# Attention scores from hi and lo parts, wide projections, and a modulation vector's row sums begun two heads earlier

## The chip, the cores and the metric

The kernel runs on one core of a Trainium2 chip as one launch. The metric is the device time of that launch in microseconds (us). The engines are PE (TensorE: matmuls, with the weight loads in a row PEld of their own), DVE (VectorE), ACT (ScalarE), POOL (GpSimd) and SP (SyncE), which here only issues DMAs. Each engine runs its own instruction list in order; between engines the kernel sets and waits for semaphores.

## The reference

Two transformer blocks on `x` of 256 tokens x 1024 features, all in float32. What is computed, cut to what matters here:

```
# block 1
sh1, sc1, g1, sh2, sc2, g2 = split(silu(c) @ w_mod + b_mod, 6)      # c: 1024 values, w_mod: 1024 x 6144
hx = rms_norm(x, norm1_g) * (1 + sc1) + sh1 ; hc the same from ctx (256 tokens)
q, k, v, u, g = split(hx @ w_in) ; kc, vc from hc                   # 8 heads of 128, 2 key heads
q, k = rope(head_rms(q)), rope(head_rms(k))
attn = softmax(q @ [kc, k].T / sqrt(128)) @ [vc, v]                 # per head: 256 x 512 scores
y_a  = attn @ w_attn_out
h    = a * sigmoid(b), a, b = split(u)                              # 512 channels
y_b  = silu(layer_norm(depthwise_conv31(h))) @ w_conv_out
x    = x + g1 * ((sigmoid(g_a) * y_a + sigmoid(g_b) * y_b) @ w_out)
x    = x + g2 * conv_glu_ffn(rms_norm(x, norm2_g) * (1 + sc2) + sh2)
x    = rms_norm(x, final_g)
# block 2
h = h + 0.5 * rms_norm(swiglu(rms_norm(h)))
q_a, k_a, v_a, q_b, k_b, v_b = split(rms_norm(h) @ w_in_2)          # 8 heads of 64 each
h = h + rms_norm([norm(stick_breaking(a)), norm(chunk_band(b))] @ w_out_2)
h = h + 0.5 * rms_norm(swiglu(rms_norm(h)))
h = h + rms_norm((p @ w_ple_proj) * sigmoid(h @ w_ple_gate))
```

## The kernel before

**Products from parts.** A float32 matrix is split in a high part (a cast to the matmul type fp32r) and a low part (the float32 value minus the high part). A product is then three fast matmuls: hi x hi, hi x lo, lo x hi. For a weight chunk ACT makes the high part (`whi`, L1348) and DVE the low part (`wlo`, L1812, behind the cast); three buffers of each rotate. A few matmuls still run on plain float32 operands: the head scores (L957, `QT` x `KT`), the values (L978), transposes, and the modulation chunks (L765).

**The stream.** All large weights come in 164 chunks of 1 MB (128 x 2048 float32) through a ring of four slots, `raw0` to `raw3`. The list `STREAM` (L99 to L111) sets their order. SP issues the loads in that order (`ring`, L454): the load of chunk c waits until chunk c-4, its predecessor in the slot, is used up (`slot_free`, L447), and every later load stands behind it in SP's list. What frees a slot depends on the kind of chunk (L422 on): the DVE split (`lo_done`) for a weight chunk, the matmuls (`mod_used`, `acc_ready`) for a modulation chunk, and DVE's row sums (`mod_dot`) for a chunk of `scale2`.

**Stages.** q, u, kv and g0 (projections of block 1); eight heads; the rest of the merge (`attnout0` to `attnout3`, `g1b`, `wout`); up0, down0, up1, down1; qa, ka, va, vb, qb, kb0, kb1 with the two attentions of block 2; wout2, up2, proj, down2, gate. In PE's program a head is: scores, the values of the head before, a chunk of the modulation block `modB` (in heads 0 to 4 one, in head 7 three: `MOD_PER_HEAD`, L67), one feature tile of g (`tiles_stage`, L694), the transposes of the probabilities (`prob_transposes`, L960). The layer norm of the conformer branch is cut over heads 5 and 6: `ln_mean` on PE, then DVE's subtraction of the mean (L2113, `ln_c`), ACT's square, `ln_var` on PE in head 6 behind its scores and values (L998), rsqrt on POOL, a diagonal on DVE (L2118, `ln_diag`), its broadcast on PE (`ln_broadcast`, L1002), DVE's multiplication (L2123, `ln_n`), ACT's affine step and silu, and the cast `cvt_hi` and subtraction `cvt_lo` (L2094) in head 7, which `conv_products` (L1015) multiply.

**DVE in the heads** (L2087 on): two row maxima (L2090), taps of the depthwise convolution (`conv_taps`, 124 in all, in units of one instruction), two reciprocals of the row sums (L2099), more taps, the low part of the last head's values (`pv_lo`, L2074), the split of the next g chunk (`splits_to`). The taps stand wherever DVE would have had room: `conv_taps(2, 7, 8, 12)` between the units of kv, then up to 16 in each head until they are used up.

**The second scale.** `sc2` is not multiplied on PE. POOL loads `c` to all partitions (`c_row`, L592); ACT takes its sigmoid; DVE multiplies (L2139); then `mod_dots` (L1911) forms for each half of a `scale2` chunk a product and its row sum in one instruction (L1919), eight in all, four chunks in the stream just ahead of `attnout1`, `wout` 0, `wout` 3 and `up0` 0.

**Projections of block 2.** `project2` (L1130) uses `tiles_stage`: for each of two chunks eight k steps of two output tiles of three parts, 48 matmuls of 256 columns; the result stands in one PSUM bank and ACT copies it (`qk_out`, L1672).

## Time and profile before

| | us |
|---|---|
| time, median of 3 runs (lowest, highest) | 981.22 (981.05, 981.88) |
| the profiled execution: its own time | 981.24 |
| its span, first to last instruction in the trace | 979.3 |
| what lies around the span | 1.9 |
| PE busy | 959.9 (98%) |
| DVE, ACT, POOL busy | 690.7 (71%), 484.2 (49%), 56.7 (6%) |
| granted TensorE clock, mean (1 is full) | 0.999 |
| from HBM | 188.35 MB, 193 GB/s over the span |

PE is busy nearly throughout; the slices of the page show tenths, and PE stands at 9 in all but the first and the last. DVE's low slices lie in the later stages; in the first third, where the heads are, its slices read 8 and 9. The chain that ended last is made of matmuls. A busy share says nothing of what a stage waits for: an engine that is 71% busy over the span can be the last one in one stage.

### The profile page before, as it was taken

To read this page: it belongs to the slowest core of one execution; us is meant where nothing else is said; L and a number is where in the kernel's file an instruction comes from. 1 tells how busy PE (TensorE), PEld (TensorE's weight loads), DVE (VectorE), ACT (ScalarE), POOL (GpSimd) and SP (SyncE) were. 2 spreads that over 40 slices of the span, in tenths; PEclk is the share of its full clock that TensorE was granted. 3 is DMA by queue.
4 is the path that set the end of the run, shared out by engine and by line. 5 is a ranking of instruction groups with operands and counts; after the bars stand their busy time and mean duration, and the time that the engine had idled before them with its cause. 6 is when DMAs were issued, how large, how long until landed. Compare 5 with 4: busy or idle time off the path is not lost.

```text
span 979.3 us, 14504 instructions
## 1 busy us (share of the span) xinstructions
PE 959.9 (98%) x5720; PEld 824.2 (84%) x5720; DVE 690.7 (71%) x895; ACT 484.2 (49%) x644; POOL 56.7 (6%) x92
## 2 busy tenths in 40 slices
PE   7999999999999999999999999999999999999997
PEld 4697788788988888889888888898988988888885
DVE  3689998479879999757777764465555667776454
ACT  3565466664355555324545433258853454443343
POOL 0251000000000000010000000101001000000000
PEclk9999999999999999999999999999999999999999
DMA  9954254466475555943665555183421654555511
GB/s 379 394 212 169 103 218 154 167 248 231 154 298 195 212 193 208 326 174 119 247 245 205 184 207 210 44 306 137 171 87 44 237 215 172 213 212 182 207 44 43
DMA packets 27842, 190.12 MB, mean 194 GB/s; under 512 B 3120, under 2 KB 3376, under 8 KB 5776
## 3 DMA queue, kind: packets, MB, share of 16 engines
q1 hardware_dynamic: 26192, 184.23, 50.8%
q0 software_dynamic: 1456, 5.12, 1.7%
q8 instruction: 36, 0.59, 0.2%
q14 instruction: 14, 0.11, 0.0%
q10 hardware_dynamic: 144, 0.07, 0.0%
HBM read 188.35 MB, written 1.05 MB: 193 GB/s over the span
## 4 chain that ended last, share of the span: by engine, by line
PE 52%; DVE 1%; POOL 0%; ACT 0%; issue 0%; DVEq 0%; POOLq 0%; ACTq 0%
PE acc L1085 15%; PE acc L1088 8%; PE acc L672 6%; PE acc L674 6%; PE acc L673 6%; PE acc L814 3%; PE acc L675 1%; PE acc L677 1%; PE acc L676 1%; PE acc L797 1%; PE acc L1234 0%; DVE X L2326 0%; DVE XN L1838 0%; DVE XN L1843 0%; PE acc L1147 0%
## 5 line engine op out<-in xcount | busy, mean ns | idle before, releaser
L1812 DVE TENSOR_TENSOR wlo<-raw,whi 128x2048 fp32r<-128x2048 f32 x135 | 308.3, 2289 | 145.5 <-ACT whi L1348 145.4
L1348 ACT CAST whi<-raw 128x2048 fp32r<-128x2048 f32 x139 | 263.2, 1906 | 126.1 <-PE acc L674 84.0
L1085 PE MATMUL acc<-x_parts,whi 128*128 128x512 f32 x960 | 301.8, 396 | 0.0
L1088 PEld LDWEIGHTS acc<-x_parts,wlo 128*128 128x128 f32 x960 | 180.3, 188 | 42.6
L1088 PE MATMUL acc<-x_parts,wlo 128*128 128x256 f32 x960 | 188.7, 278 | 0.0
L1085 PEld LDWEIGHTS acc<-x_parts,whi 128*128 128x128 f32 x960 | 146.2, 189 | 0.0
L672 PE MATMUL acc<-whi,h_hi 128*128 128x512 f32 x264 | 103.0, 390 | 0.0
L674 PE MATMUL acc<-whi,h_lo 128*128 128x512 f32 x264 | 102.7, 389 | 0.0
L673 PE MATMUL acc<-wlo,h_hi 128*128 128x512 f32 x264 | 102.7, 389 | 0.0
L675 PE MATMUL acc<-x_parts,whi 128*128 128x256 f32 x288 | 83.2, 289 | 0.0
L677 PE MATMUL acc<-x_parts,wlo 128*128 128x256 f32 x288 | 81.5, 283 | 0.0
L676 PE MATMUL acc<-x_parts,whi 128*128 128x256 f32 x288 | 81.5, 283 | 0.0
L2240 DVE TENSOR_REDUCE FULL<-acc 128x512 f32<-128x1024 f32 x60 | 73.0, 1216 | 0.0
L672 PE MATMUL acc<-whi,x_parts 128*128 128x512 f32 x168 | 67.8, 403 | 2.5 <-issue 0.8
L674 PE MATMUL acc<-whi,x_parts 128*128 128x512 f32 x168 | 65.6, 390 | 0.0
L673 PE MATMUL acc<-wlo,x_parts 128*128 128x512 f32 x168 | 65.6, 390 | 0.0
L814 PE MATMUL acc<-FULL,raw 128*128 128x128 f32 x512 | 58.8, 275 | 0.0
L675 PEld LDWEIGHTS acc<-x_parts,whi 128*128 128x128 f32 x288 | 55.2, 192 | 4.1 <-issue 3.9
L814 PEld LDWEIGHTS acc<-FULL,raw 128*128 128x128 f32 x512 | 58.1, 192 | 0.5 <-DVE FULL L1882 0.2
L674 PEld LDWEIGHTS acc<-whi,h_lo 128*128 128x128 f32 x264 | 49.6, 188 | 10.3
L673 PEld LDWEIGHTS acc<-wlo,h_hi 128*128 128x128 f32 x264 | 49.6, 188 | 10.2
L672 PEld LDWEIGHTS acc<-whi,h_hi 128*128 128x128 f32 x264 | 49.6, 188 | 10.0
(297 smaller groups left out, 1220.4 us busy)
## 6 DMA issues: line engine op xcount, KB each, us to landing
raw<-in_stream SPq DMA_DIRECT2D x164, 1024.0 KB, 4.8
early<-in_early SPq DMA_DIRECT2D x8, 1024.0 KB, 13.4
X<-in_x SPq DMA_DIRECT2D x2, 512.0 KB, 4.5
G<-in_ctx SPq DMA_DIRECT2D x1, 1024.0 KB, 21.2
...
```

Source lines behind the costliest of these rows:

```text
L672: pe.matmul(out, xh, wh, start=start, stop=False)
L673: pe.matmul(out, xh, wl, start=False, stop=False)
L674: return pe.matmul(out, xl, wh, start=False, stop=stop)
L675: pe.matmul(out, wh, xh, start=start, stop=False)
L676: pe.matmul(out, wh, xl, start=False, stop=False)
L677: return pe.matmul(out, wl, xh, start=False, stop=stop)
L814: mm = pe.matmul(acc[:, BANK[i], o * T + t * P:o * T + (t + 1) * P], w[:, k, o * P:(o + 1) * P], FULL[:, k, t * P:(t + 1) * P], start=(k = ...
L1085: pe.matmul(acc[:, BANK[i + q] + o, :], w[0][:, k, o * P:(o + 1) * P], xs[:, k, :], start=(k == 0), stop=False)
L1088: mm = pe.matmul(acc[:, BANK[i + q] + o, T:2 * T], w[1][:, k, o * P:(o + 1) * P], xhi[:, k, :], start=False, stop=(k == KD - 1))
L1348: act.copy(whi[si_slot][:, :], raw[raw_slot][:, :]).then_inc(s["hi_done"], 1)
L1812: dve.tensor_tensor(wlo[slot][:, :], raw[raw_slot][:, :], whi[slot][:, :], ALU.subtract)\
L2240: dve.tensor_reduce(dst.rearrange("p (o n) -> p o n", o=2), parts, AX, ALU.add)\
```

## The change

1. **Scores from parts.** ACT casts `QT` to `side_hi` in two instructions and writes the keys straight to a high part (`KTh`, laid over `cvt_hi`); DVE makes the low parts in two (`q_lo`) and four (`k_lo`) instructions, between taps. `scores` calls `product`, three matmuls for each one before, and waits for `q_lo` and `k_lo`. Ten of the taps before head 0 move into the heads.
2. **Head 0.** ACT copies head 0's transposed probabilities before it casts the g3 chunk, not behind.
3. **silu(c).** In place of the sigmoid behind the heads, ACT takes exp(-c) in head 2 and DVE in head 5 adds 1, takes the reciprocal of 128 x 1024 values, and multiplies by c, ahead of the subtraction of the mean.
4. **Row sums of scale2.** The four chunks stand ahead of `convout1`, `modB.5`, `attnout1` and `wout` 0; the row sums are taken in head 6 (two, one on each side of the multiplication L2123), in head 7 (two), behind `branch_b` and behind `attnout1`.
5. **Merge.** The splits of `attnout0` and `attnout1` stand further ahead, and the diagonal of the gate moves from ahead of `attnout0`'s merge to behind it.
6. **Wide projections** for ka, qb and kb0 (five chunks): the high weight is multiplied with both parts of x at once (512 columns), the low weight with the high part (256 columns), in two banks; ACT copies one half and DVE adds the other (`qk_rest`).

```diff
-for _name, _chunks in (("scale2", (("attnout1", 0), ("wout", 0), ("wout", 3), ("up0", 0))),
+for _name, _chunks in (("scale2", (("convout1", 0), ("modB.5", 0), ("attnout1", 0), ("wout", 0))),
...
+            pool.wait_ge(s["q_lo"], 2)
+            pool.dma_start(bc[:, 1, :], bcast(a["c_row"], D)).then_inc(s["c_in"], 16)
             pool.wait_ge(s["ln_ve"], 1)
...
             def scores(h):
-                        pe.wait_ge(s["q_t"], 8)
+                        pe.wait_ge(s["k_lo"], 4)
...
-                    pe.matmul(tp[:, t, :], QT[:, h, t * P:(t + 1) * P], KT[:, h // 4, :], start=True, stop=True)\
-                        .then_inc(s["sc_ready"], 1)
+                    pe.wait_ge(s["q_lo"], h // 4 + 1)
+                    product(tp[:, t, :], side_hi[:, h, t * P:(t + 1) * P], side_lo[:, h, t * P:(t + 1) * P],
+                            KTh[:, h // 4, :], KTl[:, h // 4, :], True, True, True).then_inc(s["sc_ready"], 1)
...
+            def wide_stage(si, i, n=None):
...
+                    for o in range(2):
+                        pe.matmul(acc[:, BANK[i] + o, :], w[0][:, k, o * P:(o + 1) * P], xs[:, k, :], start=(k == 0),
+                                  stop=False)
+                    for o in range(2):
+                        mm = pe.matmul(acc[:, BANK[i] + o, T:2 * T], w[1][:, k, o * P:(o + 1) * P], xhi[:, k, :],
+                                       start=False, stop=(k == KD - 1))
...
+            for j in range(2):
+                act.copy(side_hi[:, 4 * j:4 * j + 4, :], QT[:, 4 * j:4 * j + 4, :]).then_inc(s["q_hi"], 1)
...
-                if h < 7:
+                if 0 < h < 7:
                     splits_to(SPLIT["g2"] + h + 2)
...
+                if h == 0:
+                    splits_to(SPLIT["g2"] + 2)
+                if h == 2:
+                    act.wait_ge(s["c_in"], 16)
+                    act.activation(XN[:, 0, :], bc[:, 1, :], ACT.Exp, scale=-1.0).then_inc(s["c_sig"], 1)
...
+                    act.wait_ge(s["sc_ready"], TT * NH)
                     act.copy(cvt_hi[:, :, :], QT[:, 0:4, :]).then_inc(s["ln_hi"], 1)
...
-                conv_taps((2, 7, 8, 12)[u - 4])
+                if u < 7:
+                    conv_taps((2, 7, 6)[u - 4])
+                if u == 5:
+                    k_lo(4)
+                    k_lo(5)
+            conv_taps(2)
+            q_lo(0)
+            conv_taps(2)
+            k_lo(6)
+            k_lo(7)
+            q_lo(1)
...
                 if h == 5:
+                    dve.wait_ge(s["c_sig"], 1)
+                    dve.tensor_scalar(XN[:, 0, :], XN[:, 0, :], 1.0, None, ALU.add).then_inc(s["c_sig"], 1)
+                    dve.wait_ge(s["c_sig"], 2)
+                    dve.reciprocal(XN[:, 0, :], XN[:, 0, :]).then_inc(s["c_sig"], 1)
+                    dve.wait_ge(s["c_sig"], 3)
+                    dve.tensor_tensor(bc[:, 1, :], bc[:, 1, :], XN[:, 0, :], ALU.mult).then_inc(s["c_row"], 1)
                     bank_ready(ACC["ln_mean"])
...
-            splits_to(SPLIT["g2"] + 9)
-            dve.wait_ge(s["c_sig"], 1)
-            dve.tensor_tensor(bc[:, 1, :], bc[:, 1, :], XN[:, 0, :], ALU.mult).then_inc(s["c_row"], 1)
+            splits_to(SPLIT["attnout0"] + 1)
             pv_lo(NH - 1)
             mod_out("modB")
-            splits_to(SPLIT["attnout0"] + 1)
-            dve.wait_ge(s["mod_out"], MOD_N["modB"])
-            diagonal(xn2[:, D:2 * D], 0)
+            splits_to(SPLIT["attnout0"] + 2)
             branch_b(2)
-            dve.wait_ge(s["c_row"], 1)
-            mod_dots("scale2", 0)
             branch_b(3)
+            mod_dots("scale2", 2)
...
+                if j == 0:
+                    dve.wait_ge(s["mod_out"], MOD_N["modB"])
+                    diagonal(xn2[:, D:2 * D], 0)
```

**Order, DVE before head 0.** Before, from the last rotation of a key unit to the reciprocals of head 0 (L2010 and L2017 belong to the unit, L2048 is a tap, L1812 the split of the g2 chunk, L2090 the row maxima):

```order
L2048 SCALAR_TENSOR_TENSOR XN<-conv_x,vt,XN 128x256 [waits conv_dve] x8
L2010 TENSOR_TENSOR FULL<-acc,small 128x256 [waits q_rot,q_ri]
L2017 TENSOR_TENSOR FULL<-FULL,G 128x256 [waits q_tps,q_norm]
L2048 SCALAR_TENSOR_TENSOR XN<-conv_x,vt,XN 128x256 [waits conv_dve] x12
L1812 TENSOR_TENSOR wlo3<-raw0,whi3 128x2048 [waits hi_done]
L2090 TENSOR_REDUCE small<-acc 128x1 [waits sc_ready] x2
L2048 SCALAR_TENSOR_TENSOR XN<-conv_x,vt,XN 128x256 [waits conv_dve] x4
L2099 RECIPROCAL small<-small 128x1 [waits p_exp] x2
```

After, the same stretch (L2101 is a tap, L2123 `q_lo`, L2129 `k_lo`, L1862 the split, L2166 the row maxima):

```order
L2063 TENSOR_TENSOR FULL<-acc,small 128x256 [waits q_rot,q_ri]
L2070 TENSOR_TENSOR FULL<-FULL,G 128x256 [waits q_tps,q_norm]
L2101 SCALAR_TENSOR_TENSOR XN<-conv_x,vt,XN 128x256 [waits conv_dve] x2
L2123 TENSOR_TENSOR side<-QT,side 128x4x256 [waits q_hi]
L2101 SCALAR_TENSOR_TENSOR XN<-conv_x,vt,XN 128x256 [waits conv_dve] x2
L2129 TENSOR_TENSOR cvt_lo<-acc,cvt_hi 128x2x128 [waits q_t] x2
L2123 TENSOR_TENSOR side<-QT,side 128x4x256 [waits q_hi]
L1862 TENSOR_TENSOR wlo3<-raw0,whi3 128x2048 [waits hi_done]
L2166 TENSOR_REDUCE small<-acc 128x1 [waits sc_ready] x2
L2101 SCALAR_TENSOR_TENSOR XN<-conv_x,vt,XN 128x256 [waits conv_dve] x4
L2176 RECIPROCAL small<-small 128x1 [waits p_exp] x2
```

Twelve taps in a row ahead of the split have become four, with two `q_lo` and two `k_lo` among them.

**Order, DVE in heads 5 and 6.** Before, from the split at the end of head 5 (L1812) over `ln_c` (L2113), head 6's maxima and reciprocals, the copy of the variance (L2106) and the split of the g7 chunk to the multiplication `ln_n` (L2123):

```order
L1812 TENSOR_TENSOR wlo1<-raw3,whi1 128x2048 [waits hi_done]
L2113 TENSOR_TENSOR XN<-XN,acc 128x1024 [waits acc_ready]
L2090 TENSOR_REDUCE small<-acc 128x1 [waits sc_ready] x2
L2099 RECIPROCAL small<-small 128x1 [waits p_exp] x2
L2074 TENSOR_TENSOR side<-acc,side 128x256 [waits a_hi]
L2106 COPY small<-acc 128x2 [waits acc_ready]
L1812 TENSOR_TENSOR wlo2<-raw0,whi2 128x2048 [waits hi_done]
L2118 TENSOR_SCALAR XN<-consts,small 128x128 [waits ln_r]
L2118 TENSOR_SCALAR XN<-consts,small 128x128
L2123 TENSOR_TENSOR XN<-XN,acc 128x1024 [waits ln_c,acc_ready]
```

After (L1862 is the split, L2190 to L2194 the three steps of silu(c), L2196 `ln_c`, L2201 the diagonal, L1968 a row sum):

```order
L1862 TENSOR_TENSOR wlo1<-raw3,whi1 128x2048 [waits hi_done]
L2190 TENSOR_SCALAR XN<-XN 128x1024 [waits c_sig]
L2192 RECIPROCAL XN<-XN 128x1024 [waits c_sig]
L2194 TENSOR_TENSOR bc<-bc,XN 128x1024 [waits c_sig]
L2196 TENSOR_TENSOR XN<-XN,acc 128x1024 [waits acc_ready]
L2166 TENSOR_REDUCE small<-acc 128x1 [waits sc_ready] x2
L2176 RECIPROCAL small<-small 128x1 [waits p_exp] x2
L2150 TENSOR_TENSOR side<-acc,side 128x256 [waits a_hi]
L2183 COPY small<-acc 128x2 [waits acc_ready]
L1862 TENSOR_TENSOR wlo2<-raw1,whi2 128x2048 [waits hi_done]
L2201 TENSOR_SCALAR XN<-consts,small 128x128 [waits ln_r]
L2201 TENSOR_SCALAR XN<-consts,small 128x128
```

Three instructions of 128 x 1024 have come between the split and `ln_c`. The row sum L1968 follows the diagonal, then L2208, the new line of `ln_n`, and then the second row sum, which is the one that gives slot `raw0` back.

**Order, SP's loads.** Before, the loads of chunks 24 to 31: `convout1`, `modB.5` to `modB.7`, `attnout0`, the first `scale2` chunk, `attnout1`, `attnout2`; a wait is for what frees the slot, the use of the chunk four places earlier:

```order
L456 DMA raw0<-in_stream 128x2048 [waits lo_done]
L456 DMA raw1<-in_stream 128x2048 [waits mod_used]
L456 DMA raw2<-in_stream 128x2048 [waits lo_done]
L456 DMA raw3<-in_stream 128x2048 [waits lo_done]
L456 DMA raw0<-in_stream 128x2048 [waits lo_done]
L456 DMA raw1<-in_stream 128x2048 [waits mod_used]
L456 DMA raw2<-in_stream 128x2048 [waits mod_used]
L456 DMA raw3<-in_stream 128x2048 [waits acc_ready]
```

After, chunks 24 to 32: `scale2` 0, `convout1`, `scale2` 1, `modB.5` to `modB.7`, `attnout0`, `scale2` 2, `attnout1`:

```order
L473 DMA raw0<-in_stream 128x2048 [waits lo_done]
L473 DMA raw1<-in_stream 128x2048 [waits mod_used]
L473 DMA raw2<-in_stream 128x2048 [waits lo_done]
L473 DMA raw3<-in_stream 128x2048 [waits lo_done]
L473 DMA raw0<-in_stream 128x2048 [waits mod_dot]
L473 DMA raw1<-in_stream 128x2048 [waits lo_done]
L473 DMA raw2<-in_stream 128x2048 [waits mod_dot]
L473 DMA raw3<-in_stream 128x2048 [waits mod_used]
L473 DMA raw0<-in_stream 128x2048 [waits mod_used]
```

The load of `modB.6` waited for the split of the g7 chunk (third row of before), and now waits for the first two row sums, which stand in head 6 of DVE's list (fifth row of after). `modB.7` and `attnout0` stand behind it, and `attnout0` waits for the third and fourth row sum besides.

## Rows read from the trace of the kernel before

**Rows 1.** Page, part 1: busy us (share of span) and instructions.
```profile
PE 959.9 (98%) x5720; PEld 824.2 (84%) x5720; DVE 690.7 (71%) x895; ACT 484.2 (49%) x644; POOL 56.7 (6%) x92
```

**Rows 2.** Windows, PE: stretch, us, busy (instructions), PEclk, DMA, GB/s.
```profile
383.00:430.00 47.00, 47.00 (x209) 1.00 0.88 300
647.44:659.03 11.59, 11.59 (x99) 1.00 0.95 379
```

**Rows 3.** Timeline, PE at start: start, us, line, tiles, count, idle.
```profile
5.14 3.91 PE L891 MATMUL acc<-consts 128*128 128x128 f32 x20 [5.14 <-DMA consts<-in_consts]
```

**Rows 4.** Timeline, PE, heads 6 and 7.
```profile
177.36 1.84 PE L998 MATMUL acc<-consts,QT 128*128 128x1 f32 x16
...
185.34 1.04 PE L966 MATMUL acc<-consts,FULL 128*128 128x128 f32 x8
186.21 1.88 PE L957 MATMUL acc<-KT,QT 128*128 128x512 f32 x4
187.93 1.89 PE L978 MATMUL acc<-FULL,V 128*128 128x256 f32 x8
189.75 2.78 PE L765 MATMUL acc<-raw,sct 128*32 128x512 f32 x24
192.83 0.39 PE L675 MATMUL acc<-cvt_hi,whi 128*128 128x256 f32 x1 [0.29 <-DVE cvt_lo L2094]
```

**Rows 5.** Timeline, DVE, before head 0's first row maxima.
```profile
104.09 4.83 DVE L2048 SCALAR_TENSOR_TENSOR XN<-conv_x,vt,XN 128x256 f32<-128x256 f32 x12
108.85 2.28 DVE L1812 TENSOR_TENSOR wlo<-raw,whi 128x2048 fp32r<-128x2048 f32 x1
```

**Rows 6.** Timeline, ACT, head 0: the cast of the g3 chunk.
```profile
115.72 1.91 ACT L1348 CAST whi<-raw 128x2048 fp32r<-128x2048 f32 x1
```

**Rows 7.** Waits, DVE, 98 to 174.4: us in total, times, longest.
```profile
DVE wlo L1812 <- ACT whi L1348: 3.0, 6, 1.4
DVE XN L2113 <- PE acc L989: 1.8, 1, 1.8
DVE side L2074 <- ACT side L1517: 1.3, 1, 1.3
DVE FULL L2010 <- POOL small L528: 1.3, 1, 1.3
DVE small L2099 <- ACT FULL L1530: 0.8, 2, 0.5
```

**Rows 8.** Timeline, DVE, the layer norm in heads 5 and 6.
```profile
173.24 1.22 DVE L2113 TENSOR_TENSOR XN<-XN,acc 128x1024 f32<-128x1024 f32 x1 [1.78 <-PE acc L989]
...
183.05 0.48 DVE L2118 TENSOR_SCALAR XN<-consts,small 128x128 f32<-128x128 f32 x2
```

**Rows 9.** Lines, DVE by form: busy us, mean ns, idle before.
```profile
L1919 DVE CUSTOM_DVE_ANT_0 XN<-raw,bc,vt 128x1024 f32<-128x1024 f32 x16 | 20.5, 1283 | 0.3
...
L2099 DVE RECIPROCAL small<-small 128x1 f32<-128x1 f32 x16 | 2.0, 153 | 3.5 <-ACT FULL L1530 3.5
...
L1933 DVE TENSOR_TENSOR modv<-vt,acc 128x4 f32<-128x4 f32 x8 | 1.3, 158 | 6.8 <-PE acc L848 6.8
...
L2405 DVE RECIPROCAL small<-small 128x4 f32<-128x4 f32 x4 | 0.7, 171 | 0.0
...
L1907 DVE TENSOR_TENSOR mod<-vt,acc 128x16 f32<-128x16 f32 x1 | 0.2, 159 | 0.0
```

**Rows 10.** Line L456, two chunks issued at 229.3 and 229.7.
```profile
DMA to landing us min/median/max: 4.8/5.9/6.9
```

**Rows 11.** Timeline, PE, attnout0's first steps, attnout1's start, the gate's broadcast.
```profile
208.12 0.63 PE L1051 MATMUL acc<-side,whi 128*128 128x512 f32 x2
...
208.81 0.63 PE L1051 MATMUL acc<-side,whi 128*128 128x512 f32 x2
...
214.72 0.73 PE L1051 MATMUL acc<-side,whi 128*128 128x512 f32 x2 [0.86 <-DVE wlo L1812]
...
220.41 1.88 PE L1061 MATMUL acc<-XN,consts 128*128 128x512 f32 x4
```

More of the change, by code:

```diff
@@ L122 @@
 WHOLE = {"q": 1, "up0": 2, "up1": 2, "up2": 2, "qa": 2}
+WIDE = ("ka", "qb", "kb0")
 UP_FIRST = {"up0": 2, "up1": TP, "up2": 2}
@@ L155 @@
         _free = 2
+    if _name in WIDE:
+        _free = (_free + 1) // 2 * 2 % NR
+        for _ in range(_na):
+            BANK.append(_free)
+            _free = (_free + 2) % NR
+        continue
+    if _name == "kb1":
+        BANK.append(1)
+        _free = 2
+        continue
     if _name.startswith("band"):
@@ L168 @@
 UP_ACC = {ACC[_name] + _j for _name in UP_BANKS for _j in range(2, 22)}
+UP_ACC |= {ACC[_name] + _j for _name, _, _na in STAGES if _name in WIDE for _j in range(_na)}
 UP_ACC |= {ACC[f"attnout{_j}"] for _j in range(4)}
@@ L303 @@
 ss_ready ri_ready xn_ready bt_act bt_dve xf_act xf_dve bx_hi bx_lo xt_ps shift_dve xhi xlo
-q_ss v_done q_ri q_norm q_rot q_tps q_t
+q_hi q_lo k_lo q_ss v_done q_ri q_norm q_rot q_tps q_t
 glu_sig conv_in conv_dve ln_c ln_sq ln_ve ln_r ln_diag ln_n ln_y ln_hi ln_lo
@@ L1128, in _ @@
             ffn_down(1)
+            def wide_stage(si, i, n=None):
+                chunk_ready(si)
+                bank_free(i)
+                w = [r[si % NR][:, :].rearrange("p (k n) -> p k n", k=KD) for r in (whi, wlo)]
+                for k in range(KD):
+                    if n is not None and k % 2 == 0:
+                        x_ready(n, k // 2)
+                    for o in range(2):
[4 more added lines that the diff above has]
+                                       start=False, stop=(k == KD - 1))
+                mm.then_inc(s["acc_ready"], 1)
             def project2(name, n=None):
                 for j in range(2):
-                    tiles_stage(SPLIT[name] + j, ACC[name] + j, n=n if j == 0 else None)
+                    wide_stage(SPLIT[name] + j, ACC[name] + j, n if j == 0 else None)
             sp4 = full2[:, 0:GH * SC].rearrange("p (h n) -> p h n", h=GH)
@@ L1539, in _ @@
                     pv_hi(h - 1)
-                if h < 7:
+                if 0 < h < 7:
                     splits_to(SPLIT["g2"] + h + 2)
-                else:
+                if h == 6:
+                    act.activation(small[:, 158:159], minus_half, ACT.Silu)
+                if h == 7:
                     act.wait_ge(s["g_raw"], NH)
@@ L1672, in qk_out @@
             def qk_out(w, name, tiles=range(2)):
-                for n, j in enumerate(tiles):
+                for j in tiles:
+                    n = 0 if name.startswith("kb") else j
                     bank_ready(ACC[name] + n)
+                    if name in WIDE:
+                        act.activation(qk2t[w][:, 2 * j:2 * j + 2, :],
+                                       acc[:, BANK[ACC[name] + n]:BANK[ACC[name] + n] + 2, 0:T], ACT.Copy,
+                                       scale=HD2 ** -0.5 if w % 2 == 0 else 1.0).then_inc(s["qk_hi"], 1)
+                        continue
                     act.activation(qk2t[w][:, 2 * j:2 * j + 2, :],
@@ L1727, in _ @@
             stick_ln(1)
+            qk_out(2, "qb", (0,))
             splits_to(SPLIT["wout2"])
@@ L2348, in _, with qk_rest @@
             sp4 = full2[:, 0:GH * SC].rearrange("p (h n) -> p h n", h=GH)
+            def qk_rest(w, name, first, tiles=(0, 1)):
+                for j in tiles:
+                    i, at = ACC[name] + j, qk2t[w][:, 2 * j:2 * j + 2, :]
+                    bank_ready(i)
+                    dve.wait_ge(s["qk_hi"], first + j + 1)
+                    dve.scalar_tensor_tensor(at, acc[:, BANK[i]:BANK[i] + 2, T:2 * T],
+                                             HD2 ** -0.5 if w % 2 == 0 else 1.0, at, ALU.mult, ALU.add)\
+                        .then_inc(s["qk2"], 1)
             def stick_softplus(g):
```

61 lines of the change are left out of this document (39 added, 22 removed).

## The prediction

> **What bounds the kernel now.** I read the page's busy shares first: PE works for 959.9 of 979.3 us of span, DVE for 690.7 [rows 1]. So time is saved only where PE has less to issue (the wide projections, the scores) and lost wherever PE is made to stand still. Then the windows: a stage of products from parts, with its chunks coming fastest, has PE busy for 47.00 us of 47.00 at clock 1.00 with DMA at 0.88, and a projection stage for 11.59 of 11.59 [rows 2]. There is no wait to mend in them, only instructions to save. The place where the change works is the heads and the merge. There I read DVE's waits first: from 98 us to the start of the mean's subtraction they sum to 3.0+1.8+1.3+1.3+0.8 = 8.2 us in 76 [rows 7]. DVE is thus nearly full in the heads though it has a quarter of the span free, and this slack of 8.2 us is what all that is added there must fit in. The subtraction `ln_c` starts at 173.24 and ends at 174.46 [rows 8], and PE takes up `ln_var`, which needs it through ACT's square, at 177.36 without a wait [rows 4]. So `ln_c` may come 2.9 us less the square (about 1.2 with its hand-over) = some 1.6 us late before PE notices.
>
> **Scores from parts.** A head's two scores take PE from 186.21 to 187.93, 1.72 us for the two products of 512 columns [rows 4]. After, they are six matmuls of 512 columns on fp32r. Their price: a step of `attnout0`, two of 512 and two of 256 columns, takes 208.81 - 208.12 = 0.69 [rows 11]; a 256-column one is 0.121 (below), so one of 512 is (0.69 - 0.24)/2 = 0.225, and the 209 of the window above give 47.00/209 = 0.225 too. I take 0.227 with a little for the change of operands: 6 x 0.227 = 1.36: 0.36 less per head, at most 2.9 over eight. The parts cost ACT two casts in front of head 0 and DVE four `k_lo` and two `q_lo`. DVE's 12 taps of 256 columns take 4.83, 0.40 each, so 256-column `k_lo` is some 0.34 to 0.40, and `q_lo` of 1024 columns about 1.15, by the subtraction of 1024 at 1.22 and the split of 2048 at 2.28 [rows 5, 8]: 4 x 0.34 + 2 x 1.15 = 3.7 us more for DVE. Head 0's start doesn't suffer: ten taps (4.0 us) leave its approach. They are not gone, they stand in the heads, head 5 has 9 where it had none, so the DVE work up to `ln_c` grows by the whole 3.7.
>
> **Head 0's order.** ACT's cast of the g3 chunk (1.91, from 115.72 [rows 6]) now stands behind the copies of the probabilities. PE's values(0) comes some 0.3 earlier; DVE's split, which waits for the cast, loses about 2.1 us of its slack.
>
> **silu(c).** Exp on ACT in head 2 lies in ACT's free half (49% busy [rows 1]). DVE gets an addition (0.7), the reciprocal of 1024 values per partition (R) and a product (1.22, as in [rows 8]). The trace has no such reciprocal. From below: R is 1.2, if it streams like the 1024-column subtraction. Small ones: 153 ns with one element, 171 with four, so 18 ns for three, 6 ns each, while a product of 4 elements takes 158 and one of 16 takes 159 [rows 9]; at the 1.19 ns per element of the large ones, 12 elements should have cost 14 ns, so up to 13 ns hide in what is fixed. The reciprocal's three elements are then 18 to 31 ns, 6 to 10.3 each: R is 6.3 to 10.7. I take the middle, 8.5, and keep 1.2 and 10.7 as ends. The Trainium skill ("VectorE: DVE Perf Modes", the section on why there are 8 slices) says that reciprocal is an iterative divide with a repeat count of 8; by it the sum would stand where my middle puts it. The small reciprocals of this trace agree with a slope far above one pass per element.
>
> **`ln_c` comes late.** Added to DVE ahead of it: 3.7 + 0.7 + 1.2 + R = 5.6 + R. Of the 8.2 us of waits, some 6.1 will still be there (1.3 for POOL, 0.8 for the row sums' exp, 2.1 for the moved cast, some 0.8 in small pieces, 1.1 at the cast in head 5), since a later DVE doesn't shorten what it waits for at those places; about 2.1 are used up. So `ln_c` ends at C = 174.46 + 5.6 + R - 2.1 = 178.0 + R = 186.5. PE, done with head 5 some 0.5 earlier than before, stands at `ln_var` from about 176.9 to C+1.3 = 187.8, 11 us. The chain behind it has no slack: `ln_var`, POOL's root and the g7 split bring the diagonal's end, as now, to C+9.1 (183.05 + 0.48 - 174.46 [rows 8]); then a row sum of 1.28 [rows 9], and `ln_n` of 1.2 to C+11.6.
>
> **The slot that waits for row sums.** The second row sum stands behind `ln_n`: C+12.9. Only then does SP load `modB.6`, which lands 4.8 us later, and `modB.7` behind it (a pair: 4.8 to 6.9 [rows 10]), at about C+20. PE gets `ln_bc` after the diagonal to C+9.6, then the transposes (1.0), scores(7) (1.4), values(6) (1.9) and `modB.5`, a third of 2.78 [rows 4], so it is done at about C+14.5 and waits for both; with a chunk's eight matmuls behind the landing, 0.9 less what overlaps, conv_products begins at C+20.5, and as POOL's load of `final_g` shares the DMA then, I take C+21.5. Before, it began at 192.83 [rows 4] = C_before + 18.4. This adds 3.1. At the first idle of the trace, 5.14 us, the next 20 small matmuls take 3.91, against 1.04 for 8 of them at 185.34 (the mean clock granted is 1 elsewhere) [rows 3, 4]: per matmul 0.195 against 0.130, so 20 lose some 1.3 us. The gap of 11 us should cost about as much once; this stands in the 21.5. The Trainium skill ("TensorE: Matmul & The Clock Gate") says that an idle PE falls to 1.2 GHz and is warmed up again by work; the 5 us at the start agree, no later gap of the trace is long enough to test it.
>
> **Merge.** `attnout1` waits for a DVE split: it starts at 214.72 after 0.86 of idle [rows 11], so about 1 us. It goes. But the gate's diagonal (8 small instructions; two of the form take 0.48, so up to 1.9 [rows 8]) stands behind two `branch_b`, two row sums (2.7), a split, the merge, another split and `x_lo`; PE needs it at g1b. From `attnout0`'s start to g1b's is 12.3 now (220.41 - 208.12 [rows 11]); adding the DVE chain from that start gives 13.0. Net 0.7 more, and below nothing (-1.0) if DVE has cleared those row sums before `attnout0` starts.
>
> **Wide projections.** Two chunks of the present form take 11.59 us [rows 2], 5.80 for the 48 matmuls of one, 0.121 each. The new form is that of `attnout0`, eight steps of 0.69 to 0.70 [rows 11]: 5.58. Five chunks save 5 x 0.22 = 1.1 us. DVE's five additions (0.69 each) and the paired banks are hidden by the products that follow in these stages; if the cover at the stick scores failed it would cost 0.7.
>
> **Sum**, against the profiled execution (981.24, its span 979.3 and 1.9 around it; the median is 981.22, the same): late `ln_c` 178.0 + 8.5 - 174.46 = 12.0; modulation chunks 3.1; merge 0.7; projections -1.1. The scores' gain in heads 0 to 5 is lost in the wait at `ln_var`, that of 6 and 7 is in the chain's times. Together 14.7: **995.9 us**.
>
> **Rivals.**
> 1. *A reciprocal that streams.* R = 1.2, same chain: 6.2 + 1.2 = 7.4, less the 1 us of clock, +6.4, 987.7. For it: nothing else of 1024 columns takes over 1.3. Against it: the slope of the small ones. 0.14.
> 2. *The slow end of R*, 10.7: 998.1. I count it in the forecast's case.
> 3. *DVE has more slack than I left it*: all 8.2 us of waits fill, C is 2 to 4 earlier, and the taps moved into the heads meet no backlog. With R = 1.2: -2.9 scores, -0.3 head 0, -1.1 projections, +2.8 slots, +0.7 merge = -0.8, 980.4, no change. With a long R this can't be. 0.06.
> 4. *Everything hides* (the other side: faster). The second row sum comes early enough that `modB.6` lands while PE works on g7 and head 7: then -2.9, -0.3, -1.1, -1.0 = -5.3, 976. It decides at one point: C+12.9+4.8 must lie before PE's arrival at `modB.6`. For it: the heads' PE work is elastic. Against it: DVE orders the row sum behind `ln_n`, and PE's own path from `ln_n` to `modB.6` holds only scores(7), values(6) and `modB.5`, 4.2 us, under the 4.8 of a landing, and the row sum comes 1.3 behind `ln_n`, so the slot stalls PE in every case with this order. 0.05.
> 5. *The slack hides more of a long R than I think*: R 6.3 and C lower by 2: 991. It lies in my own range.
>
> **Chances.** Forecast (R long, 989 to 999.5) 0.75; streaming reciprocal 0.14; no change 0.06; faster 0.05. What a measurement of this kernel can tell from no change is about 0.2%, 2 us. So faster 0.05, same 0.06, slower 0.89. The range for 8 in 10 leaves out the two small cases and the lower part of the first rival: 987 to 999.
>
> **What would show it.** After: a RECIPROCAL of 128x1024 in head 5 of some 8.5 us on DVE (1.2 proves rival 1); PE idle by about 11 us in front of `ln_var`, released by ACT's square; PE waiting for a landing DMA at the `modB.6` and `modB.7` chunks, some 5 us; score products as six rows of 0.23 per head; no wait at `attnout1`, and one before g1b of under 1 us on DVE's diagonal; ka, qb, kb0 with 32 matmuls in 5.6 us each. I am wrong if the gap at `ln_var` is below 3 us, or if PE doesn't wait at `modB.6`.

## The result and the profile after

| | before | after |
|---|---|---|
| time, median (lowest, highest), 4 runs each | 981.41 (981.05, 981.88) | 1003.0 (1001.81, 1003.56) |
| ratio, 95% interval | | 1.0218 (1.0206 to 1.0231) |
| span of the profiled execution | 979.3 | 1001.5 |
| PE busy | 959.9 (98%) | 965.4 (96%) |
| DVE busy | 690.7 | 704.3 |
| mean granted clock | 0.999 | 0.987 |

The change costs 21.6 us. 14.5 were forecast, with 999 as the upper end, so the time lies outside the range. The page of the changed kernel, busy times as in [rows 1], and the slices of PE and of its clock:

```profile
PE 965.4 (96%) x5656; PEld 828.2 (83%) x5656; DVE 704.3 (70%) x908; ACT 486.7 (49%) x647; POOL 57.0 (6%) x92
...
PE   7999999679999999999999999999999999999997
...
PEclk9999999789999999999999999999999999999999
```

PE's lower share stands in slices 8 and 9 of the 40 (175 to 225 us), and the clock is lower in the same two. The waits of PE, of which the first two and the fourth are new:

```profile
PE acc L1017 <- ACT G L1558: 8.4, 1, 8.4
PE acc L783 <- DMA raw<-in_stream: 5.9, 2, 3.0
PE acc L909 <- DMA consts<-in_consts: 5.0, 1, 5.0
PE acc L1080 <- DVE XN L2156: 2.0, 1, 2.0
```

L1017 is `ln_var`, L783 the modulation chunks, L1080 the broadcast of the gate. (The named releaser of the first, an ACT copy of g, stands right behind the square in ACT's list, and `ln_var` needs its bank; what is late is the square's input from DVE.) DVE from the end of head 5 to the second row sum, which answers to [rows 8]:

```profile
174.77 0.69 DVE L2190 TENSOR_SCALAR XN<-XN 128x1024 f32<-128x1024 f32 x1
175.49 6.55 DVE L2192 RECIPROCAL XN<-XN 128x1024 f32<-128x1024 f32 x1
182.08 1.23 DVE L2194 TENSOR_TENSOR bc<-bc,XN 128x1024 f32<-128x1024 f32 x1
183.22 1.22 DVE L2196 TENSOR_TENSOR XN<-XN,acc 128x1024 f32<-128x1024 f32 x1
...
192.87 0.48 DVE L2201 TENSOR_SCALAR XN<-consts,small 128x128 f32<-128x128 f32 x2
193.26 1.28 DVE L1968 CUSTOM_DVE_ANT_0 conv_x<-raw,bc,vt 128x1024 f32<-128x1024 f32 x1
...
197.71 1.22 DVE L2208 TENSOR_TENSOR XN<-XN,acc 128x1024 f32<-128x1024 f32 x1 [3.16 <-PE acc L1026]
198.85 1.28 DVE L1968 CUSTOM_DVE_ANT_0 conv_x<-raw,bc,vt 128x1024 f32<-128x1024 f32 x1
```

The subtraction of the mean ends at 184.44 instead of 174.46 [rows 8]. PE at the same places, answering to [rows 4] and [rows 11]:

```profile
186.06 3.57 PE L1017 MATMUL acc<-consts,QT 128*128 128x1 f32 x16 [8.40 <-ACT G L1558]
...
205.66 1.06 PE L783 MATMUL acc<-raw,sct 128*32 128x512 f32 x8 [3.00 <-DMA raw<-in_stream]
209.59 1.94 PE L783 MATMUL acc<-raw,sct 128*32 128x512 f32 x8 [2.87 <-DMA raw<-in_stream]
...
241.17 3.68 PE L1080 MATMUL acc<-XN,consts 128*128 128x512 f32 x4 [2.04 <-DVE XN L2156]
```

The same 16 matmuls of `ln_var` took 1.84 and take 3.57; of the two modulation chunks one takes 1.06 and the next 1.94; the broadcast took 1.88 and takes 3.68. Each stands behind a wait. The windows of PE over these stretches (us, busy, instructions, granted clock, DMA share, GB/s) say why:

```profile
186.00:193.00 7.00, 6.95 (x32) 0.50 0.00 0
194.00:203.00 9.00, 8.65 (x62) 1.00 0.20 69
206.00:214.00 8.00, 5.13 (x28) 0.57 1.01 416
216.00:240.00 24.00, 23.10 (x158) 1.00 0.50 195
241.00:245.00 4.00, 3.83 (x6) 0.57 0.74 283
```

0.50 is 1.2 GHz, 1.00 is 2.4. The clock fell three times: within the wait of 8.40, within the wait of 2.87 that follows the one of 3.00, and just behind the wait of 2.04 (1.00 from 240 to 241, 0.50 from 242). Each time it stayed low while PE was already busy again.

Where the 22.2 us of span came from, by the start of the same PE work in both traces:

| first matmul of | before | after | later by | added in the stretch |
|---|---|---|---|---|
| `ln_mean` (head 5) | 171.32 | 171.74 | 0.4 | 0.4 |
| `ln_var` | 177.36 | 186.06 | 8.7 | 8.3 |
| the convolution's output, first chunk | 192.83 | 211.46 | 18.6 | 9.9 |
| `attnout0` | 208.12 | 227.82 | 19.7 | 1.1 |
| the gate's broadcast | 220.41 | 241.17 | 20.8 | 1.1 |
| `wout` | 233.27 | 255.85 | 22.6 | 1.8 |
| end of the span | 979.3 | 1001.5 | 22.2 | -0.4 |

Nothing is lost after `wout`. In the stretch of 9.9: `ln_var` 1.7 and the g7 tile 1.75 at the low clock, 5.9 of waits for the loads, about 0.9 for `modB.7` at the low clock, less 0.3 from the scores and transposes.

### The profile page after: what moved, and what is told of

Same layout as the page of the kernel before. It is cut to its first block, busy times and chain, and to the rows that moved or that the text cites. A ratio compares the mean times of both kernels' runs of the same rounds, so it can differ in the third digit from the quotient of the medians.

```text
span 1001.5 us, 14423 instructions
## 1 busy us (share of the span) xinstructions
PE 965.4 (96%) x5656; PEld 828.2 (83%) x5656; DVE 704.3 (70%) x908; ACT 486.7 (49%) x647; POOL 57.0 (6%) x92
## 4 chain that ended last, share of the span: by engine, by line
PE 50%; DVE 1%; DMA 1%; ACT 0%; issue 0%; POOL 0%; DVEq 0%; POOLq 0%; ACTq 0%
PE acc L1104 15%; PE acc L1107 7%; PE acc L690 6%; PE acc L692 6%; PE acc L691 6%; PE acc L832 3%; PE acc L1158 1%; DMA raw<-in_stream 1%; PE acc L1161 1%; PE acc L815 1%; PE acc L1269 0%; DVE X L2406 0%; DVE XN L1888 0%; DVE XN L1893 0%; PE acc L1182 0%
## 5 line engine op out<-in xcount | busy, mean ns | idle before, releaser
L1862 DVE TENSOR_TENSOR wlo<-raw,whi 128x2048 fp32r<-128x2048 f32 x135 | 308.6, 2291 | 143.0 <-ACT whi L1383 142.9
L1107 PE MATMUL acc<-x_parts,wlo 128*128 128x256 f32 x960 | 188.6, 278 | 0.0
L1104 PEld LDWEIGHTS acc<-x_parts,whi 128*128 128x128 f32 x960 | 146.2, 189 | 0.0
L693 PE MATMUL acc<-x_parts,whi 128*128 128x256 f32 x208 | 60.8, 292 | 0.0
L694 PE MATMUL acc<-x_parts,whi 128*128 128x256 f32 x208 | 59.6, 287 | 0.0
L695 PE MATMUL acc<-x_parts,wlo 128*128 128x256 f32 x208 | 59.6, 286 | 0.0
L2101 DVE SCALAR_TENSOR_TENSOR XN<-conv_x,vt,XN 128x256 f32<-128x256 f32 x120 | 49.7, 477 | 0.0
## 6 DMA issues: line engine op xcount, KB each, us to landing
early<-in_early SPq DMA_DIRECT2D x8, 1024.0 KB, 12.9
```

The source lines that it names most:

```text
L693: pe.matmul(out, wh, xh, start=start, stop=False)
L694: pe.matmul(out, wh, xl, start=False, stop=False)
L695: return pe.matmul(out, wl, xh, start=False, stop=stop)
L1104: pe.matmul(acc[:, BANK[i + q] + o, :], w[0][:, k, o * P:(o + 1) * P], xs[:, k, :], start=(k == 0), stop=False)
L1107: mm = pe.matmul(acc[:, BANK[i + q] + o, T:2 * T], w[1][:, k, o * P:(o + 1) * P], xhi[:, k, :], start=False, stop=(k == KD - 1))
L1862: dve.tensor_tensor(wlo[slot][:, :], raw[raw_slot][:, :], whi[slot][:, :], ALU.subtract)\
```

## The experiments

My theory: two chains, one behind the other. DVE's reciprocal holds up `ln_c` and so `ln_var`; then the load of `modB.6` waits for the second row sum; each wait lowers the clock behind it. The rival: one of them alone sets the time, and the other only moves it. The time of before beside the first four was 981.32 (15 runs).

**e1_short_recip**, the changed kernel but for one line:

```diff
-                    dve.reciprocal(XN[:, 0, :], XN[:, 0, :])
+                    dve.reciprocal(XN[:, 0, 0:P], XN[:, 0, 0:P])
```

> The changed kernel with the reciprocal on 128 of its 1024 columns (the other columns keep 1+exp(-c), so that vector's values are left wrong). My theory, that the reciprocal holds up the mean's subtraction and PE behind it: the reciprocal falls from 6.55 us to 0.15 + 128 x 0.0063 = 1.0, the wait at ln_var from 8.4 to 2.9, and the time from 1003.0 by 5.6 to 997.4; if the shorter gap also leaves TensorE's clock at full, another 3.5 less, 994. Rival, that the loads queued behind the row sums set the time and the reciprocal only moves the wait: within 1 us of 1003.

Measured: 996.4 us (993.6 to 998.4), 1.0156 (1.0137 to 1.0175), 6.6 less than the changed kernel. The reciprocal of 128 columns takes 0.95 us, and the wait at `ln_var` is 2.79. The rival falls.

**e2_old_slots**, the changed kernel with the places of before for the row sums:

```diff
-for _name, _chunks in (("scale2", (("convout1", 0), ("modB.5", 0), ("attnout1", 0), ("wout", 0))),
+for _name, _chunks in (("scale2", (("attnout1", 0), ("wout", 0), ("wout", 3), ("up0", 0))),
...
-                    mod_dot("scale2", 0, 0)
...
-                    mod_dot("scale2", 0, 1)
...
             branch_b(2)
+            dve.wait_ge(s["c_row"], 1)
+            mod_dots("scale2", 0)
             branch_b(3)
```

> The changed kernel with the four scale2 chunks and the eight row sums back in their places of before, silu(c) through exp kept in head 5. My theory: the waits for the loads of modB.6 and modB.7 go (5.9) and the half clock behind them (0.9 in the chunk, 1.1 in the convolution's projection), together 7.9 less: 995.1; the wait at ln_var stays 8.4. Rival, that the row sums were hidden and all comes from the reciprocal: 1003 and the wait for the loads still there or replaced by one as long.

Measured: 993.1 us (992.7 to 994.8), 1.0125 (1.011 to 1.0141). That is 9.9 less than the changed kernel, 2 more than expected. PE's waits:

```profile
PE acc L1017 <- ACT G L1558: 8.4, 1, 8.4
PE acc L909 <- DMA consts<-in_consts: 5.1, 1, 5.1
PE acc L1080 <- DVE XN L2156: 2.0, 1, 2.0
```

The wait for the loads is gone, the other two stand as they were. But the clock did not fall behind the wait of 2.0 this time:

```profile
233.12 1.98 PE L1080 MATMUL acc<-XN,consts 128*128 128x512 f32 x4 [2.03 <-DVE XN L2156]
```

From the broadcast to `wout` it is 12.98 us here, 14.68 in the changed kernel and 12.86 before. These 1.7 us are the rest of the saving, and the new places of the row sums do not explain them.

**e3_old_slots_short**, both edits.

> Both edits at once: old places of scale2 and a reciprocal of 128 columns. If the two costs add: 1003.0 - 7.9 - 5.6 = 989.5. If a gap of 2.9 us before ln_var leaves the clock at full: 986. If the costs hide each other (either alone would do): not below 993.

Measured: 986.75 us (985.8 to 987.7), 1.0053 (1.0037 to 1.0068): 16.25 less than the changed kernel. Alone the edits gave 6.6 and 9.9, together 16.5. The two costs add, as far as the clock at the broadcast lets one tell: its four matmuls took 3.64 in e1, 1.98 in e2 and 2.76 in e3, behind the same wait of 2.0. Of e1 and e3 the same matmuls are worth a look, first of e1, then of e3:

```profile
180.66 1.97 PE L1017 MATMUL acc<-consts,QT 128*128 128x1 f32 x16 [2.79 <-ACT G L1558]
```

```profile
179.69 3.57 PE L1017 MATMUL acc<-consts,QT 128*128 128x1 f32 x16 [2.79 <-ACT G L1558]
```

After the same wait of 2.79 the clock was still full in e1 and already half in e3. In e1 it fell behind `ln_var` (0.74 from 181 to 184). e1's times scatter over 5 us, where those of before lie within 1.7; that the clock does this is not shown, as the run of 998.4 has nearly the mean clock of the run of 995.2 (0.991 and 0.992).

**e4_no_scale2**: silu(c) by the sigmoid and the row sums both as before; parts 1, 2, 5 and 6 of the change stay.

```diff
-                    act.activation(XN[:, 0, :], bc[:, 1, :], ACT.Exp, scale=-1.0).then_inc(s["c_sig"], 1)
...
+            act.activation(XN[:, 0, :], bc[:, 1, :], ACT.Sigmoid).then_inc(s["c_sig"], 1)
             splits_to(SPLIT["attnout0"] + 1)
...
-                    dve.tensor_scalar(XN[:, 0, :], XN[:, 0, :], 1.0, None, ALU.add).then_inc(s["c_sig"], 1)
-                    dve.wait_ge(s["c_sig"], 2)
-                    dve.reciprocal(XN[:, 0, :], XN[:, 0, :]).then_inc(s["c_sig"], 1)
```

> The changed kernel without its silu and scale2 parts: sigmoid, product, chunks and row sums as before; scores from parts, head 0's order, the later diagonal and the wide projections stay. My theory: DVE is 3.7 us fuller, its waits take most of it, no wait at ln_var over 0.5; scores give 1.5 to 2.9, the wide projections 0.4, the merge costs what it costs in the changed kernel, 2.9 (wait of 2.0 at g1b less 0.9, and 1.8 of low clock): 981.4 - 2 - 0.4 + 2.9 = 982, between 980 and 983.5. Rival, that the scores' parts overload DVE by themselves: above 984 with a wait at ln_var of over 2.

Measured: 983.25 us (981.4 to 985.4, 11 runs), 1.0019 (1.001 to 1.0028). There is no wait at `ln_var` (176.98, 0.4 earlier than before), so the low parts of q and k alone don't overload DVE. But at the gate's broadcast:

```profile
221.70 2.07 PE L1079 MATMUL acc<-XN,consts 128*128 128x512 f32 x2 [2.54 <-DVE XN L2152]
```

The broadcast's four matmuls took 3.57. Here the runs themselves show both clocks: the three with a mean clock of 0.999 took 981.4, 981.6 and 982.0, the other eight, at 0.997 or 0.998, took 982.7 to 985.4. This kernel has shed 19.75 of the 21.6 us. What it still has too much is in the merge.

**e5_diag_old**, e4 with the diagonal back, and `attnout1`'s split as well:

```diff
             mod_out("modB")
-            splits_to(SPLIT["attnout0"] + 2)
+            dve.wait_ge(s["mod_out"], MOD_N["modB"])
+            diagonal(xn2[:, D:2 * D], 0)
             branch_b(2)
...
-                if j == 0:
-                    dve.wait_ge(s["mod_out"], MOD_N["modB"])
-                    diagonal(xn2[:, D:2 * D], 0)
```

> The last kernel of the first set (no silu and scale2 parts) with the gate's diagonal back ahead of the merge, the two splits still early. If the diagonal behind two splits, the merge and x_lo is what PE waits for at g1b: its 2.5 us go, and the low clock behind them (1.4 in the broadcast's matmuls), and attnout1 still has no wait: 983.25 - 3.9 = 979.3. Rival, that the wait at g1b only moves to attnout1 (the split comes 1.65 later): 982 or more.

The edit does more than the expectation says. The split of `attnout1` does not stay early: it goes back behind `branch_b(3)`, so that DVE's merge is that of before. (`attnout0`'s split never moved: `SPLIT["g2"] + 9` of before and `SPLIT["attnout0"] + 1` of after are the same chunk.)

Measured: 980.5 us (980.0 to 981.9), 0.9994 (0.9985 to 1.0003). 2.7 less than e4, not 3.9: the wait at the broadcast is gone, and one stands at `attnout1`:

```profile
214.59 0.73 PE L1069 MATMUL acc<-side,whi 128*128 128x512 f32 x2 [0.97 <-DVE wlo L1858]
```

That is the wait of before [rows 11], with the split in the place of before; whether the diagonal by itself makes it, this run can't say (e9 does). So in the merge the change had traded 0.9 us here for 2.0 there, and for the clock.

**e6_head0_old**, e5 with head 0 as before:

```diff
-                if 0 < h < 7:
+                if h < 7:
                     splits_to(SPLIT["g2"] + h + 2)
...
-                if h == 0:
-                    splits_to(SPLIT["g2"] + 2)
```

> As e5_diag_old, and ACT's cast of the g3 chunk again ahead of head 0's copies. Theory: that cast's new place delays all of ACT's and DVE's work in heads 1 and 2 (waits of 0.38 and 1.08 at the transposes and values(1)); with it back they go and the wait of 0.3 at values(0) returns: 1.0 to 1.2 less than e5_diag_old, 978.2. Rival, that the backlog comes from DVE's extra 3.7 us: within 0.3 of e5_diag_old, both waits still there.

Measured: 979.6 us (978.1 to 980.2), 0.9983 (0.9974 to 0.9992), 1.0 less than e5 as expected, from a base that was 1.2 higher. The waits of 0.38 and 1.08 in heads 1 and 2 are gone; one of 1.2 stands at values(0), where 0.3 was expected. So part 2 of the change costs 1 us.

**e7_scores_only**, the kernel before with part 1 alone.

> The kernel before with the scores from parts alone (with the casts, the low parts and the taps moved into the heads). If DVE's slack takes the 3.7 us: 8 x 0.3 to 0.36 less = 2.4 to 2.9, less 0.3 for the cast of the convolution's input that now waits for the last scores: 978.7. If the low parts overload DVE: 981 or more, with waits of PE in the heads or at ln_var.

Measured: 980.2 us (979.5 to 981.3), 0.9989 (0.998 to 0.9998): a gain of about 1, not 2.5. By the starts in its trace each head gains 0.25 at the scores and 0.08 at the transposes, 2.6 in eight heads. Against it 0.94 is lost once at values(0) and 0.34 once at the convolution's output:

```profile
119.49 1.97 PE L983 MATMUL acc<-FULL,V 128*128 128x256 f32 x8 [1.18 <-issue]
```

So shorter scores ahead of ACT's copies of head 0 only lengthen this wait. The copies even come later than before (118.32 instead of 117.54), because DVE reaches head 0's maxima 8.4 us behind the last key unit's rotation instead of 7.8; 0.7 of this is a wait of the last `k_lo` pair for ACT. The forecast had said that head 0's start doesn't suffer.

**e8_dots_first**, the changed kernel with one line moved:

```diff
                     mod_dot("scale2", 0, 0)
+                    mod_dot("scale2", 0, 1)
                     bank_ready(ACC["ln_bc"])
...
                         .then_inc(s["ln_n"], 1)
-                    mod_dot("scale2", 0, 1)
```

> The changed kernel with the second row sum of the first scale2 chunk directly behind the first one, ahead of the multiplication ln_n, where DVE waited 3.16 us for PE. Theory, that the load of modB.6 waits for this row sum in DVE's order: it is issued at 195.8 instead of 200.1, lands about 201.3, before PE wants it (202.5), and modB.7 about 205.2: the two waits of 5.9 fall to about 1.7, the chunk after them runs at full clock: 1003.0 - 4.2 - 2 = 997. Rival, that the transfers are late because the DMA is shared with final_g and the following chunks: waits of over 4 us stay.

Measured: 994.0 us (993.0 to 996.0), 1.0137 (1.0121 to 1.0152). 9.0 less than the changed kernel, where 6 was expected. The load of `modB.6` is issued at 194.8 instead of 200.2, PE waits for no chunk, and the windows over the chunks and what follows are at full clock:

```profile
194.00:203.00 9.00, 9.00 (x70) 1.00 0.75 287
203.00:209.00 6.00, 5.88 (x53) 1.00 0.90 355
209.00:215.00 6.00, 5.97 (x46) 1.00 0.84 352
```

DMA is 0.75 to 0.90 busy and nobody waits: the place of one 1.28 us instruction in DVE's order is what made PE wait for these loads. Not all of the 9.0 is its direct work. The broadcast ran at full clock here, as in e2 (1.98 behind a wait of 2.05), which is 1.7 of it. And the two loads landed sooner, `modB.6` and `modB.7` of the changed kernel first, then of e8:

```profile
DMA to landing us min/median/max: 5.4/7.2/9.0
DMA to landing us min/median/max: 4.7/5.8/6.9
```

In the changed kernel they start at 200.2, together with POOL's load of `final_g`; in e8 that load comes 4.5 us behind them. That it is what slows them is likely and not tested by itself.

The last four ask for the best version, beside 981.28 of before.

**e9_diag_mid**, e6 with the diagonal between the split and `branch_b(2)`. As e6 had the split late, what moves is the split, to ahead of the diagonal:

```diff
             mod_out("modB")
+            splits_to(SPLIT["attnout0"] + 2)
             dve.wait_ge(s["mod_out"], MOD_N["modB"])
             diagonal(xn2[:, D:2 * D], 0)
             branch_b(2)
```

> As e6_head0_old, with the gate's diagonal between attnout1's split and branch_b(2), so behind the split and ahead of the row sums. In e6 the split behind the diagonal left PE 0.99 us at attnout1; in e4 the diagonal behind the merge left it 2.5 us at g1b. With neither: no wait at either place, 1.0 less than e6: 978.6. If the DVE chain to the next split is what counts, the wait moves to attnout2 and the time is that of e6.

Measured: 979.5 us (978.7 to 980.0), 0.9981 (0.9972 to 0.999), the same as e6; 978.6 was expected. PE first, then DVE:

```profile
214.08 0.70 PE L1069 MATMUL acc<-side,whi 128*128 128x512 f32 x2 [1.08 <-DVE G L2202]
```

```profile
213.25 0.68 DVE L2202 TENSOR_TENSOR G<-acc,G 128x512 f32<-128x512 f32 x1
```

The wait is as long, but its releaser is now `branch_b(3)`, which stands behind the diagonal and two row sums and gives back the second of the two banks that `attnout1` writes. In e4, with the split early and no diagonal ahead of it, there was no wait here. So the 1.65 us of the diagonal reach PE by `branch_b(3)` if the split is early, and by the split if it is late.

**e10_ka**, e9 with `qk_rest` for ka's first pair ahead of the second va split.

```diff
-            splits_to(SPLIT["va"] + 2)
-            qk_rest(1, "ka", 0)
+            splits_to(SPLIT["va"] + 1)
+            qk_rest(1, "ka", 0, (0,))
+            splits_to(SPLIT["va"] + 2)
+            qk_rest(1, "ka", 0, (1,))
```

> As e9, and DVE adds ka's first pair of banks before the split for the second va chunk instead of behind it. The wait of 0.2 to 0.4 in front of va goes: from ka's first matmul to va's first 11.25 us instead of 11.57. In the time that is 0.3, hardly to be told: 978.3; the trace decides.

Measured: 979.5 us (979.2 to 981.6), 0.9985 (0.9976 to 0.9994), not to be told from e9. The trace decides: from ka's first matmul to va's it is 11.23 us in e10, but 11.23 in e9 too, against 11.57 in the changed kernel. The wait ahead of va had gone before this edit, which thus tested nothing.

**e11_g2_split**, e10 with `splits_to(SPLIT["g2"] + 1)` behind head 0's maxima.

> As e10, and DVE's split of the g2 chunk behind head 0's row maxima instead of ahead of them. Theory: the maxima come 1.5 us earlier, so exp, scaling and ACT's copies of head 0, and the wait of 1.19 at values(0) goes, with nothing new behind it, since g2 is wanted 9 us later: 977.3. Rival, that ACT's cast of g3 waits for its buffer and holds the copies: unchanged against e10.

Measured: 979.8 us (978.6 to 980.3), 0.9982 (0.9973 to 0.9991), no gain. The maxima do come earlier, but the split now stands ahead of the reciprocals, which stay where they were, and ACT waits for them:

```profile
115.24 1.34 ACT L1570 ACTIVATE FULL<-FULL,small 128x512 f32<-128x512 f32 x2 [3.07 <-DVE small L2170]
```

values(0) still waits, 1.25. Neither my reason nor the rival's was right: the 2.28 us of the split lie on head 0's chain on either side of the maxima.

**e12_early_sigmoid**, e11 with the early row sums of e8, and:

```diff
-                    act.activation(XN[:, 0, :], bc[:, 1, :], ACT.Exp, scale=-1.0).then_inc(s["c_sig"], 1)
+                    act.activation(XN[:, 0, :], bc[:, 1, :], ACT.Sigmoid).then_inc(s["c_sig"], 1)
...
-                    dve.tensor_scalar(XN[:, 0, :], XN[:, 0, :], 1.0, None, ALU.add).then_inc(s["c_sig"], 1)
-                    dve.wait_ge(s["c_sig"], 2)
-                    dve.reciprocal(XN[:, 0, :], XN[:, 0, :]).then_inc(s["c_sig"], 1)
-                    dve.wait_ge(s["c_sig"], 3)
```

> As e11, but with the changed kernel's early places for the scale2 chunks and row sums (the second one directly behind the first), and silu(c) by ACT's sigmoid in head 2 with only DVE's product in head 5. It asks whether beginning the row sums early pays once the reciprocal is gone. Mine: no. The slot of modB.6 comes free with the second row sum at about 186.5 and lands at 191.5 to 192, PE wants it at 188.9: a wait of about 2.9 and one of 1 to 2 for modB.7, and some low clock: 4 to 6 above e11, 982 to 983. Rival, that the freed DVE time in the merge pays for it: below e11.

Measured: 984.4 us (983.7 to 986.5), 1.0041 (1.0027 to 1.0054), 4.6 above e11. PE:

```profile
177.01 1.95 PE L1017 MATMUL acc<-consts,QT 128*128 128x1 f32 x16 [0.86 <-ACT G L1558]
...
194.69 1.06 PE L783 MATMUL acc<-raw,sct 128*32 128x512 f32 x8 [1.88 <-DMA raw<-in_stream]
```

The wait of 1.88 is for `modB.7`; `modB.6` landed just in time, where I had expected a wait of 2.9. In e8 both were in time, since PE itself was late and slow. And the clock fell behind `ln_var`, after a wait of only 0.86:

```profile
176.00:179.00 3.00, 2.14 (x18) 1.00 0.42 178
179.00:181.00 2.00, 2.00 (x11) 0.51 0.00 0
181.00:183.00 2.00, 2.00 (x13) 0.64 0.00 0
```

Against e11, by the starts in the two traces: 1.0 up to `ln_var`, 1.6 in the g7 tile at the lower clock, 1.6 at the modulation chunks, 1.5 up to `attnout0` (granted clock 0.57 from 196 to 200), and 1.3 back from there to the broadcast, where neither of the two waits is left: the rival had that part right. So with the reciprocal gone the early places still cost about 4.6 us. Only the 1.6 at the modulation chunks is the wait for the ring's loads itself, where a slot held by row sums is one chunk less in front of PE. I did not try to put them in any other place.

Best of all are e6, e9, e10 and e11, which can't be told apart at 979.5 to 979.8, 0.15 to 0.19% below before.

## Why the prediction was wrong

The direction and the chain were right, the size was not. By its own steps:

**The reciprocal.** It takes 6.55 us. The rows gave 6.3 to 10.7 and I chose 8.5. The trace had the answer in its plainest form: 18 ns for three more elements, 6 each, 6.3 us [rows 9]. My allowance for time hidden in a small instruction was not needed: from 128 to 1024 columns it is (6553 - 952) / 896 = 6.25 ns an element. The Trainium skill ("VectorE: DVE Perf Modes", section "First, the fixed hardware budget") has reciprocal with a repeat count of 8; by that count and the 0.96 GHz that the same page gives, the slope is, as an estimate, 8.3 ns, a third above what was measured, so here the measurement decides. This term was 2 us too high.

**`ln_c` late.** The step C = 178.0 + R gives 184.55 with the measured R; the trace has 184.44. The ledger of DVE's work and waits held: of the 8.2 us of waits 6.1 were to stay, and 5.7 did, from 98 us to the end of `ln_c`:

```profile
DVE wlo L1862 <- ACT whi L1383: 3.6, 6, 1.8
DVE FULL L2063 <- POOL small L545: 1.4, 1, 1.4
DVE cvt_lo L2129 <- ACT cvt_hi L1521: 0.7, 1, 0.7
```

e3 and e4 bear it out: with the reciprocal down to 0.95 the wait at `ln_var` is 2.79, without the silu steps none. Forecast 11 us of wait, measured 8.4, from the shorter R and because PE came 0.8 later out of head 5 (177.66, not 176.9).

**The clock.** This is the step that failed. I gave the fall one us, from the loss of the first 20 matmuls of the program [rows 3], and counted one fall. There were three, and each cost more than that: `ln_var` +1.7, the g7 tile +1.75 (7.58 against 5.83 from its first matmul to the next block), `modB.7` +0.9, the convolution's first chunk +1.1, the broadcast and what follows +1.8. Together some 7 us against 1. What I did not draw is the length of a fall: at clock 0.50 the same matmuls took about twice as long here (1.84 and 3.57, 1.88 and 3.68), so a fall costs what PE's work in it takes at full clock, not a fixed price. Nor do the rows bear out my one us: the profile of the kernel before gives the granted clock over those first 20 matmuls as 1.00, so that they were slow by the clock is not shown.

```profile
5.00:9.00 4.00, 3.86 (x22) 1.00 1.02 410
```

So the 5 us at the start, which I took as the case that agrees, show nothing of the clock; the drops of the changed kernel do. The Trainium skill ("TensorE: Matmul & The Clock Gate", section "HAM oscillation — how this bites in real kernels") says that the cost is paid again at every wait that drops the clock. I used the page for one gap; the changed kernel's trace agrees with it for three (0.50 or 0.57 behind each).

**The slot that waits for row sums.** Right in mechanism (e2: -9.9, e8: -9.0), too small: the convolution was to begin at C+21.5 and began at C+27.0. Along the path of the loads: the g7 tile at half clock made `ln_bc` late, DVE waited 3.16 for it ahead of `ln_n`, and the second row sum ended at C+15.7, not C+12.9, which is 2.8. The load then took 5.5 us to land and the next chunk came 3.9 later, 9.4 for the two where I had 7.1; these 2.3 are a second term that I had too small, and they are not clock. The last chunk at half clock is the rest, less the 1 us I had allowed.

**Merge.** Forecast +0.7, measured +1.1 to the broadcast and 1.8 behind it. The wait of 0.86 at `attnout1` did go, and one of 2.04 came. From `attnout0` to the broadcast it took 13.35, where I had 13.0. The 1.8 behind is the clock: 1.7 of it goes where the clock stays up behind the same wait (e2, e8).

**Wide projections.** Forecast -1.1, measured -0.4 to -0.5. The windows of the changed kernel over ka, qb and kb0:

```profile
670.06:681.30 11.24, 11.24 (x67) 1.00 0.96 380
712.15:723.41 11.26, 11.26 (x66) 1.00 0.25 95
725.65:731.28 5.63, 5.63 (x35) 1.00 0.93 343
```

A chunk takes 5.63 against 5.80 [rows 2], 0.17 less instead of 0.22. ka's gain of 0.3 was lost again in front of va, where PE waited for DVE's additions.

**Scores.** The forecast had PE out of head 5 some 0.5 earlier than before; `ln_mean` came 0.4 later. Their gain was eaten by ACT's and DVE's order in heads 0 to 2, as e6 and e7 show.

**Rivals.** The streaming reciprocal is out by the 6.55. That everything hides is out as well. The one I should have had is that of low clock in the whole stretch: half speed for about 7 us of full-speed work where I counted 1 us.

In sum: 14.7 forecast (against the profiled execution), -1.7 at `ln_var`, +5.2 between `ln_var` and the convolution, +2.9 of low clock in the convolution's first chunk and behind the broadcast, +0.4 in the merge's chain, +0.7 for the projections: 22.2, which is what the span grew by. Of this, low clock is 2.8 by the late row sum, 0.9 in `modB.7` and the 2.9, some 6.6. Without it the time would be 996.4, inside the range of the forecast; this is an estimate from these terms.
